# Prompt attention on one NeuronCore: mask on VectorE, scaled diagonals as the second operand of the turn, values of three units back ahead of it

## The reference

```python
s_s = jnp.einsum('bqgrd,bqgkcd->bqgrkc', q, kb).astype(jnp.float32) * scale
p_s = masked_softmax(s_s.reshape(b, nq, g, r, nk), m_s.reshape(b, nq, g, 1, nk)).reshape(s_s.shape)
o_s = jnp.einsum('bqgrkc,bqgkcd->bqgrd', p_s.astype(vb.dtype), vb)
s_w = jnp.einsum('bqgrd,bkgd->bqgrk', q, kw).astype(jnp.float32) * scale
p_w = masked_softmax(s_w, m_w)
o_w = jnp.einsum('bqgrk,bkgd->bqgrd', p_w.astype(vw.dtype), vw)
return gate[..., 0:1] * o_c + gate[..., 1:2] * o_s + gate[..., 2:3] * o_w
```

## Time and profile before

| what | value |
|---|---|
| time, median of 3 runs | 1466.07 us (1464.58 to 1468.4) |
| the profiled execution, its own time | 1465.81 us |
| its span in the trace | 1464.1 us |
| granted TensorE clock, mean | 0.996 of full speed |
| PE busy | 1430.9 us (98%) |
| DVE busy | 847.9 us (58%) |
| ACT busy | 413.0 us (28%) |
| POOL busy | 211.9 us (14%) |
| attention of the prompt | about 666 to 776 us |

### The profile page before, as it was taken

How to read it: one execution, slowest core, us unless ns; L and a number is a source line. 1 busy time by engine, 2 the same in 40 slices (tenths; PEclk the granted TensorE clock), 3 DMA queues, 4 the chain that set the end, 5 groups by cost and what they waited for, 6 DMA issues and landing times.

```text
span 1464.1 us, 30419 instructions
## 1 busy us (share of the span) xinstructions
PE 1430.9 (98%) x12340; PEld 1130.4 (77%) x12340; DVE 847.9 (58%) x1649; ACT 413.0 (28%) x890; POOL 211.9 (14%) x276
## 2 busy tenths in 40 slices
PE   9999999999999999999999889999999999999997
PEld 8887578878888866775667668888888888888886
DVE  7665058633433447526774537677666766666664
ACT  3112372123333316227775631102311011101001
POOL 1000324532222224434001210000000000000000
PEclk9999999999999999999999999999999999999999
DMA  6222543211111238457003963432222222222221
GB/s 264 87 87 72 182 166 111 96 61 44 50 46 36 101 118 254 156 165 250 1 2 91 334 260 137 141 98 83 75 84 86 76 83 87 87 74 97 90 87 61
DMA packets 57399, 163.94 MB, mean 112 GB/s; under 512 B 7312, under 2 KB 19696, under 8 KB 55952
## 3 DMA queue, kind: packets, MB, share of 16 engines
q1 hardware_dynamic: 48608, 121.46, 24.9%
q0 software_dynamic: 7936, 39.40, 7.8%
q10 hardware_dynamic: 720, 1.16, 0.2%
HBM read 144.01 MB, written 22.15 MB: 113 GB/s over the span
## 4 chain that ended last, share of the span: by engine, by line
PE 91%; DVE 4%; ACT 2%; issue 1%; SPq 1%; DMA 1%; DVEq 0%; ACTq 0%
PE acc L1059 26%; PE acc L1210 17%; PE acc L1978 5%; PE acc L2006 5%; PE acc L1987 5%; PE acc L2031 4%; PE acc L1152 2%; PE acc L1332 2%; PE acc L1167 2%; PE acc L1733 2%; PE acc L1745 2%; PE acc L1756 1%; PE acc L1349 1%; PE acc L1094 1%; PE acc L1071 1%
## 5 line engine op out<-in xcount | busy, mean ns | idle before, releaser
L1059 PE MATMUL acc<-sb_work,sb_ring 128*128 128x272 f32 x602 | 150.9, 392 | 0.0
L2524 ACT ACTIVATE sb_omemT<-acc 128x272 f32<-128x272 f32 x74 | 29.3, 396 | 386.0 <-PE acc L1978 234.2
L1210 PE MATMUL acc<-sb_work,sb_ring 128*128 128x272 f32 x504 | 129.2, 398 | 4.4 <-DVE sb_work L2733 2.9
L1059 PE MATMUL acc<-sb_work 128*128 128x272 f32 x530 | 133.0, 393 | 0.0
L1059 PEld LDWEIGHTS acc<-sb_work,sb_ring 128*128 128x128 f32 x602 | 114.4, 190 | 23.6
L1059 PEld LDWEIGHTS acc<-sb_work 128*128 128x128 f32 x530 | 100.5, 190 | 21.4 <-issue 0.8
L1210 PEld LDWEIGHTS acc<-sb_work,sb_ring 128*128 128x128 f32 x504 | 93.1, 190 | 25.7 <-issue 7.1
L1978 PE MATMUL acc<-sb_work,sb_ring 128*128 128x272 f32 x308 | 77.2, 393 | 1.0 <-issue 1.0
L1987 PE MATMUL acc<-sb_work,sb_ring 128*128 128x272 f32 x308 | 77.1, 392 | 0.0
L1210 PE MATMUL acc<-sb_onsaT,sb_omemT 128*128 128x272 f32 x272 | 69.5, 399 | 0.0
L1978 PEld LDWEIGHTS acc<-sb_work,sb_ring 128*128 128x128 f32 x308 | 58.4, 190 | 13.4 <-issue 1.4
(11 more groups left out here) (495 smaller groups left out, 2787.4 us busy)
## 6 DMA issues: line engine op xcount, KB each, us to landing
sb_ring<-w_stream SPq DMA_DIRECT2D x144, 512.0 KB, 3.5
sb_work<-pages SPq DMA_DIRECT2D x56, 192.0 KB, 4.2
branch_gates<-sb_work SPq DMA_DIRECT2D x24, 272.0 KB, 2.8
sb_work<-branch_gates POOLq DMA_DIRECT2D x8, 816.0 KB, 14.7
sb_ring<-w_stream SPq DMA_DIRECT2D x16, 384.0 KB, 3.3
sb_work<-mem_kT SPq DMA_DIRECT2D x8, 512.0 KB, 7.5
sb_work<-mem_v SPq DMA_DIRECT2D x8, 512.0 KB, 9.9
query_features<-sb_work SPq DMA_DIRECT2D x10, 272.0 KB, 3.5
```

Source lines behind the costliest of these rows:

```text
L1059: mm = pe.matmul(out, w[:, q, :], x[q], start=q == 0, stop=q == n - 1)
L1210: mm = pe.matmul(acc[3][:, (7 * u + ph) % 2, 0:HALF_T], w, x, start=q == 0 and ph in (0, 1, 5), stop=q == 3, skip_group_check=True)
L2524: act.activation(keeps(u)[:, s], bank(u, (0, 3)[s]), ACT.Copy).then_inc(unit_kept, 1)
```

## The change

The mask is no longer a matmul: DVE adds it to the scores in PSUM ahead of the maximum. The exponentials are no longer scaled in place. Instead gate over sum is multiplied onto an identity, one 128 x 128 diagonal for each group and branch of the unit, and the turn becomes a plain f32 matmul of a block with its diagonal in place of a transpose with the identity. Up to unit 9 DVE makes the diagonals, from unit 10 on POOL does. On PE the values of unit u-3 now come ahead of the turn of unit u-2. DVE waits once for the last stores out of the region in which the diagonals lie.

```diff
+            for u in range(DIAG0, N_ATT):
+                nb, c = len(ATT_UNITS[u][2]), 16 * (u % 2)
+                pool.wait_ge(at_norm, u - DIAG0 + 1)
+                pool.tensor_tensor(scale_diag[:, u % 3, 0:NG * nb, :], bc(ident, 1, NG * nb),
+                                   bc(small[:, c + 12:c + 12 + NG * nb], 2, P), ALU.mult).then_inc(at_scaled, 1)
             pool.wait_ge(ma_done, MA + QT)
...
-                    pe.matmul(o[:, g], qT[gs, r, t * P:w], keys, start=True, stop=False)
-                for g in range(NG):
-                    mm = pe.matmul(o[:, g, :, t * P:w], bf_ident, bc(bf_causal, 1, nb), start=False, stop=True)
+                    mm = pe.matmul(o[:, g], qT[gs, r, t * P:w], keys, start=True, stop=True)
...
-                        mm = pe.transpose(acc[2][:, g, k * P:(k + 1) * P], probs[u % 3][:, g, k * P:(k + 1) * P], ident)
+                        mm = pe.matmul(acc[2][:, g, k * P:(k + 1) * P], probs[u % 3][:, g, k * P:(k + 1) * P],
+                                       scale_diag[:, u % 3, g * len(bs) + k // (t + 1), :], start=True, stop=True)
...
+                if N_ATT <= u < N_ATT + 2:
+                    memory_scores(u - N_ATT)
                 if u == 2:
                     pe.wait_ge(sb_done, 1)
-                if u < N_ATT:
-                    att_turn(u - 2)
                 if u == 3:
                     pe.wait_ge(sw_done, 1)
-                if N_ATT <= u < N_ATT + 2:
-                    memory_scores(u - N_ATT)
-                    att_turn(u - 2)
                 if u >= 3:
                     att_values(u - 3)
+                if u < N_ATT + 2:
+                    att_turn(u - 2)
...
+                ahead = acc[u % 2][:, :, 0:nb * w].rearrange("p g (b k) -> p g b k", b=nb)[:, :, :, t * P:w]
+                own(dve.tensor_tensor(ahead, ahead, bc(bc(const("causal"), 1, nb), 1, NG), ALU.add))
...
+                if u >= DIAG0 + 2:
+                    dve.wait_ge(at_scaled, u - 1)
+                scales = dve.tensor_tensor(rows(12).rearrange("p (g b) -> p g b", g=NG),
+                                           rows(8).rearrange("p (g b) -> p g b", g=NG), gates, ALU.mult)
...
+                if u >= DIAG0:
+                    return
+                dve.tensor_tensor(scale_diag[:, u % 3, 0:NG * nb, :], bc(ident, 1, NG * nb), bc(rows(12), 2, P), ALU.mult)\
+                   .then_inc(at_scaled, 1)
```

More of the change, by code:

```diff
@@ L331, in program @@
         late_at = at[0]
-        m_probT = [region(None, MEM_H * 2, P) for _ in range(2)]
+        scale_diag = region(late_at, 3, 2 * NG, P)
+        m_probT = [region(late_at + n * MEM_H * 2 * P, MEM_H * 2, P) for n in range(2)]
         assert at[0] <= 16800
@@ L560, in program @@
             sem, ("cs_mm", "cs_shift", "cs_exp", "cs_prob", "cs_turn", "cs_copied", "cs_out", "cs_o"))
+        at_norm = sem("at_norm")
         at_s, at_max, at_exp, at_scaled, at_turn, at_copied, at_pv, at_o = map(
@@ L682, in program @@
         HEAD_UNITS = N_ATT // HPG
+        DIAG0 = 10
         T_ATT = (T_SK, T_WK)
@@ L3027, in att_scale @@
                 own(dve.reciprocal(rows(8), rows(4)))
[L3028 to L3032, removed]
-                else:
[L3034 to L3037, removed]
+                if u >= DIAG0 + 2:
+                    dve.wait_ge(at_scaled, u - 1)
+                scales = dve.tensor_tensor(rows(12).rearrange("p (g b) -> p g b", g=NG),
+                                           rows(8).rearrange("p (g b) -> p g b", g=NG), gates, ALU.mult)
+                if u < DIAG0:
+                    own(scales)
+                else:
+                    scales.then_inc(at_norm, 1)
+                if u >= DIAG0:
+                    return
+                dve.tensor_tensor(scale_diag[:, u % 3, 0:NG * nb, :], bc(ident, 1, NG * nb), bc(rows(12), 2, P), ALU.mult)\
+                   .then_inc(at_scaled, 1)
             def att_out(r):
@@ L3044, in _ @@
             att_max(0)
+            for n in range(2):
+                dve.wait_ge(spilled[n], 16 * N_FILL // 2)
             for u in range(1, N_ATT + 1):
```

## The result

The changed kernel takes 1495.6 us (median of four runs, 1493.5 to 1497.78) against 1465.32 for the kernel before (1462.6 to 1468.4), a ratio of 1.0206 with a 95% interval of 1.0178 to 1.0234, so whether the loss is over 2% stays open. It is slower by 30.3 us; the prediction had 1496, inside a range of 1485 to 1506. The profiled execution of after took 1493.5 us with a span of 1491.8, so it stands 2.1 under its median.

The account below looks back on a forecast made before the run. The prediction took PE's own instructions to set the length of a head. Its terms, 27.0 - 5.6 - 3.5 + 8.2 + 1.0 + 1.7 + 0.5 + 1.0, summed to 30.3 us, giving 1496 us, range 1485 to 1506.

Parts of the forecast that it names:

- turn as a product: PE's turn, 40 blocks a head in 6 heads: each f32 matmul block costs 0.1125 us more, +27.0 us.
- masks off PE: Mask matmuls leave PE for DVE, 12 x 0.23 + 24 x 0.12: -5.6 us.
- waits for scaling gone: PE's turns no longer wait for DVE's scaling of the exponentials: -3.5 us.
- values wait for the copy: Values(u-3) on PE wait for ACT's copy of turn(u-3), 1.5 a head over 5.5 heads: +8.2 us, bounds 0 to 12.
- diagonal of unit b: POOL's diagonal for turn b comes slightly late, 0.2 for each of five heads: +1.0 us, bounds 0 and 3.
- diagonal of unit 10: POOL makes it after 24 page-number loads, at about 708.9; PE wants it at 707.2: one wait, +1.7 us.
- start of the stage: Mask of unit 0 before the first exponentials: 0.69 on DVE for 0.23 on PE, +0.5 us.
- last unit: Values(35) wait for their copy, with values(34) now ahead of turn 35 and not filling the wait: +1.0 us.
- copies are ready: Rival: values find ACT's copies ready and POOL is in time, 1485 to 1490 us; chance 0.18.
- POOL is late: Rival: page-number loads at 0.89 make PE wait 8.7 us, 1503, or 1505 with a later b diagonal; chance 0.12.
- PE really runs behind DVE: Rival: hidden PE idle time absorbs the doubled turn; mask and scaling waits are saved, about 1457 us; chance 0.03.
- The factor of four: Rival on the turn: by the Trainium skill's transpose rule it costs 79 us, not 27, about 1548; chance 0.02.

## Why the prediction was right

The forecast held in its mechanism. That it also held to half a microsecond in size is luck: terms were off by up to 3.3 us and cancelled.

| step | predicted | shown |
|---|---|---|
| turn as a product | +27.0 | +30.3 (5.05 a head) in after, +27.8 (4.64) alone |
| masks off PE | -5.6 | -5.6 as PE's work (0.94 a head) |
| waits for scaling gone | -3.5 | -2.8 (0.46 a head) |
| values wait for the copy | +8.2 | +7.1 (1.29 a head, 5.5 heads) |
| diagonal of unit b | +1.0 | 0: ready at 719.68 for a turn at 720.04 |
| diagonal of unit 10 | +1.7 | 0 in after; 0.97 with the old order, 5.43 with short turns |
| start of the stage | +0.5 | +1.5, the size of the slow clock |
| last unit | +1.0 | about +1 (1.19 with nothing in it) |
| sum | +30.3 | +31.5; the stage has +31.3, the program +30.3 |

**The product.** The term that was off most is this one. Per record the figure was right, 0.11. But I took a group of 8 blocks between its likes, 1.78; alone in the kernel before, with a mask in front and values behind, it takes 1.88, and in after, between values and scores, 1.98. That is 3.3 us over 36 groups, 0.09 each.

**The waits for copies** have the predicted pattern, 0.44, 0.22, 0.42, 0, 0.21, 0 against 0.42, 0.21, 0.42, 0, 0.21, 0. The 0.2 a head that I added for an ACT still busy with exponentials did not occur.

**The waits for scaling.** The prediction saw one hole in the head from 699.20 to 716.49; there are two, the second at 707.71, and six heads of 0.46 make 2.8. The 3.5 of the earlier trace rows holds the waits of the start too: its longest, 0.6, is that of the first turn, and this turn waits in after as well, 0.80 for its diagonal.

**POOL.** A load of page numbers takes 0.523, not 0.60, and a diagonal of 512 elements a row 1.04, not 1.27. The place for a wait was named rightly, and the two kernels that reach unit 10 two us sooner or more do wait there. In after PE comes to that turn at 708.93 and not at 707.2 as forecast: the products in front of it took about 0.8 more and the slow start 1.0. So the forecast wait of 1.7 was missed for two reasons, a late PE and loads that were faster than assumed.

**The start.** I had priced the mask on the path to the first exponentials, not what the clock does after idle times of PE. A clock below full speed in the stage was one of the prediction's own signs of being wrong, and it showed, at 0.83 from 666 to 676 us. It cost 1.5 us, and it is part of why PE came late to the turn of unit 10.

**The rivals.** That copies are ready fell with the first head; that POOL is late fell in after, but two experiments have it. That PE really runs behind DVE, so that a doubled turn would cost nothing, fell with the product alone: +24 us, with PE busy for 60.00 of the 60 us from 700 to 760. The factor of four fell with the same run.

No kernel here beats the one before. The two whose time can't be told from it are the mask alone (1.0007) and the change without its product and with POOL from unit 16 (1.0008). Their stages are 5.4 and 4.6 us longer, and the second leaves gate over sum out of the output, so it shows a cost and is no kernel to use.

## What to carry to other kernels

On an engine that is busy 99% of a stage, price a change by that engine's records, group by group, with the neighbours that the group will have: folding a scaling into a transpose made it an f32 product of two records a block and cost 24 us, while the pass that it removed lay almost entirely beside PE. Work moved off the full engine is a gain only if the taker isn't the one it waits for, as the mask alone shows. And a wait that is predicted from two clocks running towards each other (POOL's loads, PE's turns) moves with every other term: make the other part faster and it appears.

## What the hardware showed unexpectedly

PE's granted clock fell from 2.4 to 1.2 GHz for some 3 us after idle times of 1.93 and 0.80 us at the start of the stage, and after 0.66 and 0.96; it didn't after 0.66 and 0.74. It fell also after one idle time of 5.43 in the middle (0.94 from 700 to 760 us). The idle times of 1.93 and 0.80 come in six kernels, with slow groups behind them in all six, and 0.66 with 0.74 in two, without; 0.66 with 0.96 and the hole of 5.43 come in one profile each. Groups then take 1.8 to 1.9 times as long (1.54 to 1.58 for 0.85, 1.90 for 1.02), so a hole of 5.4 us cost 7.8; the two kernels that differ by it are 7.6 apart in the stage.

A group's length hangs on its neighbours, with no wait in the rows. For a product it is about 0.1 us for each side on which the tile shape changes. A product of 8 blocks of 128 x 128 takes 1.78 between its likes, 1.88 with a mask (128 x 128) in front and values (128 x 64) behind, and 1.98 between values and scores (64 x 128), in whichever order these stand. A mask takes 0.12 in front of a turn and 0.21 in front of values. So a mask in front of a turn was partly paid for: where it is taken out, the turn has the change of shape itself. For a transpose the two steps are 0.09 and 0.05: 8 blocks take 0.88 between likes, 0.97 with one change and 1.02 with two. In after itself two turns stand between values and the memory's scores, which have the shape of the turn. The one of 8 blocks takes 1.89:

```profile
798.46 2.05 PE L1751 MATMUL acc<-sb_work,sb_omemT 128*128 128x128 f32 x16
800.35 1.89 PE L1776 MATMUL acc<-sb_work 128*128 128x256 f32 x8
```

The rule fits these rows; a kernel made to test it was not run, and why a change of shape costs time is not shown.
